# Hybrid decoder step on one Trainium2 core: order of the sample group's memory attention and page attention

## What is computed

```python
# sample group: latent attention over 2048 cached positions in 16 pages of 128 per sequence
q_lat = einsum('bthd,chd->bthc', q_nope, w_uk)
s_past = (q_lat . lat_past + q_rope . kr_past) * scale       # 8 heads, latent 256 + rope 32
p = softmax([s_past, s_new]); o = (p . [lat_past, c_kv]) . w_uv
# sample group: memory attention, 4 heads of 128, 256 memory tokens per sequence
mem_o = softmax(qx . mem_k * X_HEAD_DIM ** -0.5) . mem_v
# both groups
h = x + (g0 * (pool_y @ w_pool_out) + g1 * (mla_o @ w_mla_out) + g2 * (mem_o @ w_x_out)) @ w_o
q = rmsnorm(h) @ w_peer_q; idx, gate = product-key top 16 of 8 heads   # 128 experts per token
y = h + sum_k gate_k * gelu(h . peer_u[idx_k]) * peer_v[idx_k]
```

## Time and profile before

| what | value |
|---|---|
| median of the runs shown | 2406.39 us |
| the profiled execution, its own time | 2412.29 us |
| its span, first to last instruction | 2410.6 us |
| granted TensorE clock, mean | 0.749 |
| moved by DMA | 688.02 MB, mean 285 GB/s |
| instructions | 22105 |

### The profile page before, as it was taken

One profiled execution on the slowest core, in us unless ns is written; L12 is line 12 of the kernel. 1 busy time (PEld: TensorE's weight loads), 2 busy tenths in 40 slices (PEclk: granted clock), 3 DMA queues, 4 the chain that ended last, 5 costly groups with the idle time before them and its releaser, 6 DMA issues.

```text
span 2410.6 us, 22105 instructions
## 1 busy us (share of the span) xinstructions
PE 1353.5 (56%) x7122; PEld 803.3 (33%) x7122; DVE 1138.8 (47%) x2797; ACT 302.5 (13%) x760; POOL 1082.1 (45%) x1182
## 2 busy tenths in 40 slices
PE   7998999894454347998743855500045510034513
PEld 5874788783232224555531611100001100001100
DVE  2104521136757743434798074078866068840060
ACT  2214520112222121001010110000000000000000
POOL 0000000005564534555466156666666676666673
PEclk9998899996776658999865876655566755567656
DMA  6212045437786979999999579999999999999996
GB/s 197 76 57 59 1 111 147 147 107 273 252 293 223 362 277 364 353 370 374 345 389 402 180 275 364 362 391 372 373 345 353 370 384 379 369 348 358 371 384 258
DMA packets 328363, 688.02 MB, mean 285 GB/s; under 512 B 39943, under 2 KB 179528, under 8 KB 328239
## 3 DMA queue, kind: packets, MB, share of 16 engines
q0 software_dynamic: 160032, 576.69, 63.6%
q1 hardware_dynamic: 168215, 109.90, 15.7%
HBM read 682.36 MB, written 4.18 MB: 285 GB/s over the span
## 4 chain that ended last, share of the span: by engine, by line
PE 34%; DVE 23%; issue 12%; another core or an unknown queue 11%; DMA 8%; POOL 5%; DVEq 3%; ACT 2%; SPq 2%; POOLq 0%; ACTq 0%
PE bank L693 26%; DVE arena L1883 15%; POOL arena L640 5%; DVEq L1819 3%; PE bank L1175 3%; PE bank L689 2%; DMA arena<-in_w_mla_out_dram 2%; DMA arena<-in_peer_v_dram,arena 2%; DMA arena<-in_cache_mem_v_dram 1%; DMA arena<-in_x_sample_dram 1%; PE bank L1150 1%; DMA arena<-in_w_pool_out_dram 1%; ACT arena L1211 1%; DVE arena L1826 1%
## 5 line engine op out<-in xcount | busy, mean ns | idle before, releaser
L640 POOL DMA_INDIRECT arena<-in_peer_u_dram,arena x544 | 514.9, 947 | 842.1 <-PE bank L693 548.1
L693 PE MATMUL bank<-arena 128*128 128x256 f32 (+7 forms) x2940 | 706.1, 397 | 103.1 <-issue 52.0
L640 POOL DMA_INDIRECT arena<-in_peer_v_dram,arena x544 | 516.2, 949 | 405.6 <-PE bank L1175 159.3
L1883 DVE CUSTOM_DVE_ANT_0 arena<-arena,bank 128x1024 f32<-128x1024 f32 x544 | 639.2, 1216 | 58.5 <-issue 50.8
L693 PEld LDWEIGHTS bank<-arena 128*128 128x128 f32 (+2 forms) x2940 | 539.2, 192 | 270.2 <-issue 103.5
L1175 PE MATMUL bank<-arena 128*32 128x512 f32 x2176 | 383.4, 842 | 317.5 <-DMA arena<-in_peer_v_dram,arena 251.4
L689 PE MATMUL bank<-arena 128*128 128x128 f32 (+5 forms) x774 | 150.3, 344 | 586.3 <-DVE arena L1900 367.2
L689 PEld LDWEIGHTS bank<-arena 128*128 128x128 f32 (+5 forms) x774 | 115.0, 176 | 636.2 <-DVE arena L1900 368.4
L1175 PEld LDWEIGHTS bank<-arena 128*32 128x32 f32 x2176 | 80.3, 136 | 597.9 <-issue 597.8
L1211 ACT ACTIVATE arena<-bank 128x256 f32<-128x256 f32 (+12 forms) x399 | 156.6, 428 | 505.1 <-PE bank L693 143.5
L1912 DVE TENSOR_TENSOR arena<-arena,bank 128x1024 f32<-128x1024 f32 x5 | 6.1, 1221 | 380.7 <-PE bank L1175 194.8
(11 more groups left out here) (142 smaller groups left out, 777.2 us busy)
## 6 DMA issues: line engine op xcount, KB each, us to landing
arena<-in_w_in_dram SPq DMA_DIRECT2D x48, 512.0 KB
arena<-in_w_peer_q_dram SPq DMA_DIRECT2D x32, 512.0 KB
arena<-in_cache_kv_latent_dram SPq DMA_DIRECT2D x86, 128.0 KB
arena<-in_peer_u_dram,arena POOLq DMA_INDIRECT x544
arena<-in_peer_v_dram,arena POOLq DMA_INDIRECT x544
arena<-in_w_o_dram SPq DMA_DIRECT2D x8, 1024.0 KB
arena<-in_w_in_dram SPq DMA_DIRECT2D x6, 1024.0 KB
arena<-in_cache_kv_latent_dram POOLq DMA_DIRECT2D x42, 128.0 KB
```

What stands on the lines that cost most here:

```text
L640: pool.indirect_dma_start(out=ring[s % RING], out_offset=None, in_=table[0], in_offset=IndirectOffsetOnAxis(ap=ix, axis=0)).then_inc(land[ ...
L693: last = pe.matmul(dst, lhs(k), rhs(k), start=(k == 0), stop=(k == n - 1))
L1883: dve.tensor_tensor_reduce(ring[s % RING], ring[s % RING], h_dot, 1.0, 0.0, ALU.mult, ALU.add, act_a[:, p % 2, k:k + 1]).then_inc(u_free, 1)
```

## The change

1. The memory attention of the 8 samples leaves the background. It now stands behind prompt_kv and ahead of the prompt's attention on TensorE, ScalarE and VectorE, and the prompt's attention waits for its end. It has 3 buffers instead of 2, loaded before the weights of part(0); a load from the fourth on waits for mem_values of the sequence that had the buffer. mem_turns(n+1) stands ahead of mem_values(n-1).
2. In the background only the pages are left ahead of part(1). page_turns(0) and its copies come first; step s then has the units (1) page_probs(s-1) and page_scores(s), (2) page_turns(s+1) with ScalarE's copies, (3) page_values(s-1), and on ScalarE step s's exponential, now behind step s+1's copies. The page buffers and what their loads wait for are as before.
3. SyncE loads 6 pages of a step and GpSimd 2, these ahead of gather 9 + 6s; GpSimd reads both page numbers at once. w_uv moves behind the last page load, into latT's place, once the last scores are done.
4. The ticks: page units 2 gathers apart (3 to 103), part(1)'s merges from 114 on, 5/2 apart, its last unit at 339 instead of 359. zw is cleared at gather 130 instead of 124.

The diff, cut to its core (the mem_ functions themselves are moved unchanged but for `% 2` becoming `% 3` on smem):

```diff
-    return (mine, []) if s < 2 else (mine[0:5], mine[5:])
+    return (mine, []) if s < 2 else (mine[0:6], mine[6:])
...
-    ticks = [u0 + 3 + 5 * i // 3 for i in range(3 * (STEPS + 1))]
-    ticks += [u0 + 90 + 2 * i for i in range(3)]
-    ticks += [u0 + 96 + 2 * i for i in range(2 * (NB + 2))]
-    ticks += [u0 + 138 + 13 * h // 5 for h in range(2 * MERGE)]
-    ticks += [u1 + 11 + 2 * r for r in range(12)]
-    ticks += [u1 + 37 + 2 * t for t in range(3)]
-    ticks += [u1 + 44 + 5 * t // 2 for t in range(3)]
-    ticks += [u1 + 52 + 3 * j for j in range(QJ + 2)]
+    ticks = [u0 + 3 + 2 * i for i in range(3 * (STEPS + 1))]
+    ticks += [u0 + 106 + 2 * i for i in range(3)]
+    ticks += [u0 + 114 + 5 * h // 2 for h in range(2 * MERGE)]
+    ticks += [u0 + 236 + 5 * r // 2 for r in range(12)]
+    ticks += [u1 + 12 + 2 * t for t in range(3)]
+    ticks += [u1 + 20 + 3 * t for t in range(3)]
+    ticks += [u1 + 32 + 3 * j for j in range(QJ + 2)]
...
             def load_memory(b):
-                if b < 2:
-                    sp.wait_ge(pv_mm, STEPS - 2 + b)
-                else:
-                    sp.wait_ge(mo_mm, b - 1)
-                    sp.wait_ge(mt_mm, 2 * (b - 1))
+                if b == 0:
+                    sp.wait_ge(pool_mm, 2 * PG)
+                    sp.wait_ge(pool_d, PG)
+                elif b >= 3:
+                    sp.wait_ge(mo_mm, b - 2)
+                    sp.wait_ge(mt_mm, 2 * (b - 2))
...
+            for b in range(NB):
+                load_memory(b)
             for n in range(4):
                 load_merge(0, n)
...
-                if s == 1:
-                    sp.dma_start(wuvs[:], ...)
-            for b in range(NB):
-                load_memory(b)
+            sp.wait_ge(ps_mm, STEPS)
+            sp.dma_start(wuvs[:], ...)
...
+            pe.wait_ge(kv_ev, KV_UNITS)
+            mem_turns(0)
+            pe.wait_ge(bank_zero, 2)
+            for n in range(NB + 2):
+                if n >= 2:
+                    mem_out(n - 2)
+                if 1 <= n <= NB:
+                    mem_probs(n - 1)
+                if n < NB:
+                    mem_scores(n)
+                if n + 1 < NB:
+                    mem_turns(n + 1)
+                if 1 <= n <= NB:
+                    mem_values(n - 1)
...
             pe.wait_ge(kv_ev, KV_UNITS)
+            pe.wait_ge(mx_ev, NB)
             pe.wait_ge(krk_done, 1)
...
+                page_turns(0)
                 for s in range(STEPS + 1):
                     if s == HALVES + 1:
                         page_out(0)
-                    if s < STEPS:
-                        page_turns(s)
-                    yield
                     if s >= 1:
                         page_probs(s - 1)
                     if s < STEPS:
                         page_scores(s)
+                    yield
+                    if s + 1 < STEPS:
+                        page_turns(s + 1)
                     yield
                     if s >= 1:
                         page_values(s - 1)
```

More of the change, by code:

```diff
@@ L378, in hybrid_step @@
         ld_pagp = [sem(f"ld_pagp{i}") for i in range(3)]
-        ld_smem = [sem(f"ld_smem{i}") for i in range(2)]
+        ld_smem = [sem(f"ld_smem{i}") for i in range(3)]
         ld_wuv = sem("ld_wuv")
@@ L846, in _, with mem_turns @@
                 prompt_kv(n)
+            def mem_turns(b):
+                pe.wait_ge(ld_smem[b % 3], 32 * (b // 3 + 1))
+                for i in range(2):
+                    if b >= 1:
+                        pe.wait_ge(mt_ev, 2 * b - 1 + i)
+                    for k in range(4):
+                        h, m = 2 * i + k // 2, k % 2
+                        last = turn(bank[:, 4 + i, k * P:(k + 1) * P],
+                                    smem[b % 3][:, 0, m, h * XD:(h + 1) * XD], P)
+                    last.then_inc(mt_mm, 1)
@@ new lines, in mem_scores, with mem_out @@
+            def mem_scores(b):
+                pe.wait_ge(mt_ev, 2 * b + 2)
+                if b >= 1:
+                    pe.wait_ge(ms_exp, b)
+                for h in range(XH):
+                    last = pe.matmul(bank[32 * h:32 * h + TS, 6, 0:MEM],
+                                     qxs[:, h, b * TS:(b + 1) * TS], smT[:, h], start=True, stop=True)
+                last.then_inc(ms_mm, 1)
+            def mem_out(b):
+                pe.wait_ge(mo_ev, b + 1)
+                if b >= 1:
+                    pe.wait_ge(mx_ev, b)
+                turn(bank[:, 7, 384:512], smo[:, b % 2], P).then_inc(mx_mm, 1)
@@ new lines, in mem_probs, with mem_values @@
+            def mem_probs(b):
+                pe.wait_ge(ms_exp, b + 1)
+                if b >= 1:
+                    pe.wait_ge(mo_ev, b)
+                if b >= 2:
+                    pe.wait_ge(mx_ev, b - 1)
+                for m in range(2):
+                    last = turn(bank[:, 7, m * P:(m + 1) * P], sms[:, b % 2, m * P:(m + 1) * P], P)
+                last.then_inc(mp_mm, 1)
+            def mem_values(b):
+                pe.wait_ge(mp_ev, b + 1)
+                if b >= 1:
+                    pe.wait_ge(mx_ev, b)
+                for m in range(2):
+                    for h in range(XH):
+                        last = pe.matmul(bank[32 * h:32 * h + TS, 7, 256:256 + XD], smpT[:, m, 32 * h:32 * h + TS],
+                                         smem[b % 3][:, 1, m, h * XD:(h + 1) * XD], start=(m == 0), stop=(m == 1))
+                last.then_inc(mo_mm, 1)
@@ L987, in page_out, with pages @@
                 last.then_inc(po_mm, 1)
[L989 to L1027, removed]
-                    pe.wait_ge(mx_ev, b)
-                for m in range(2):
-                    for h in range(XH):
-                        last = pe.matmul(bank[32 * h:32 * h + TS, 7, 256:256 + XD], smpT[:, m, 32 * h:32 * h + TS],
-                                         smem[b % 2][:, 1, m, h * XD:(h + 1) * XD], start=(m == 0), stop=(m == 1))
-                last.then_inc(mo_mm, 1)
-            def sample():
+            def pages():
                 pe.wait_ge(pq_ev, QJ)
                 pe.wait_ge(sc_ev, QJ)
+                page_turns(0)
                 for s in range(STEPS + 1):
@@ L1067, in sample @@
                 yield
-                pe.wait_ge(bank_zero, 2)
-                for n in range(NB + 2):
-                    if n >= 2:
-                        mem_out(n - 2)
-                    if n < NB:
-                        mem_turns(n)
-                    if 1 <= n <= NB:
-                        mem_probs(n - 1)
-                    yield
-                    if n < NB:
-                        mem_scores(n)
-                    if 1 <= n <= NB:
-                        mem_values(n - 1)
-                    yield
-                pe.wait_ge(mx_ev, NB)
+                pe.wait_ge(sot_ev, 1)
             def part(g):
@@ L1181, in _ @@
                 pass
-            bg = Background(joined(sample(), part(1)))
+            bg = Background(joined(pages(), part(1)))
             for p in range(TILES):
```

147 lines of the change are left out of this document (74 added, 73 removed).

## The result

The changed kernel takes 2516.18 us (median; 2507.39 to 2521.65), against 2406.8 us before (four runs; it was 2406.39 for the first three): a ratio of 1.0451, 95% interval 1.0416 to 1.0486. The forecast was 2467 us, 2408 to 2515. The direction was right, and the time lies just above the range. The profiled execution spans 2519.9 us, 109.3 more than before.

The account below looks back on a forecast made before the run. Gathers were taken to bound the kernel, paced by page steps and these by page loads. Front +62, gather stage +14, part(1) -15 made +61 us: 2473 us against the profiled 2412.3, 2467 at the median; range 2408 to 2515.

Parts of the forecast that it names:

- Part 1, the front: Memory attention moved to the front: five uncovered sequences at 8.75 us plus fill and drain, delaying the first gather 62 us.
- Part 2, the page cycle: Page stage: load, turns, values, load become one cycle, 20.0 us a step against 12.6.
- I take 13.0: Page load on SyncE with a sixth page: 13.0 us from issue until the turns start.
- 4 us each is left: Page stage: VectorE's two picks of about 20 us lie mostly beside loads, leaving 4 us each uncovered.
- they set nothing: ScalarE's page steps: exponential waits behind copies, but probabilities and scores fit inside the next load's 13 us; no cost.
- Two last steps and the start of the stage: Page stage: page_values(0) some 5 us later; two last steps without loads, 15 us; page_values(15) ends at 882.
- The first four merge units lie beside these products: Before tile 0's weights: first four merge units covered by VectorE's 21 remaining products, at about 1.3 us each.
- At its end the ticks are 20 gathers earlier ... I take 3 units: End of part(1): earlier ticks get 3 more query units done before gather 396 stops, saving 15 us.
- (a): Page stage: loads shorten without five gathers' traffic, a step keeps 12.6 us; 2371 us, chance 0.16.
- (b): Page stage and front: load 15.9 us, step 22.9, memory sequences at the old 10.8; 2515 us, chance 0.14.
- (c): Part(1)'s queries finish before gather 396, so its hold vanishes, 38 us less; 2429 us, chance 0.14.
- the signs: Trace marks: first gather near 612 us, TensorE's rope-key wait over 150, turns 18 to 22 apart, gather 396 idle 35 to 45.

Follow-up runs that it names:

- the second experiment: Kernel after with ScalarE's exponential of step s put ahead of the copies of step s + 1, TensorE's turns still ahead of values: 1.0585, 2531.87 us.

## Why the prediction came out as it did

The forecast's mechanism holds: page loads had their lookahead taken away, and the cycle load, turns, values, load sets the step. Undoing that order alone takes 1.0451 to 1.0124. The sum missed by 48 us (+61 said, +109.3 measured, both profiled). Step by step:

- **Part 1, the front: right.** +62 said, +58.3 measured; 8.75 us a sequence said, 8.2 measured. Fill and drain together were as put (18 said, 17 measured), though the "5.2 us from turns to the end of the values" was misread: 854.02 to 859.23 reaches to the next issue, and the values end at 858.56.
- **Part 2, the page cycle: the mechanism right, the load mis-sized.** "I take 13.0" for issue to turns is the step that failed. It measured 16.1 us, in the load shown and in the mean of the twelve loads whose turns show the wait (14.4 to 17.7). The reason beside it, "the engines are emptier", had it the wrong way round: six gathers are released by the same page_values as the load and run in a burst beside it, and with the gathers held back one load takes 10.1 us (761.31 to 771.44). The average DMA share did fall (0.63), but in the 16 us of the load shown it is 0.82, where the three loads of the earlier trace rows had 0.73, 1.04 and 0.88. Turns measured 4.2 (4.6 said), values 2.5 (2.4 said). The 13 steps took 294.5 us where 13 times 20.0 and 8 for the picks had been said: 26 us of the miss.
- **The picks, "4 us each is left": right or better.** In the kernel after no step with a pick stands out, while in the second experiment each does, by 8 to 10 us.
- **The exponential queued behind copies, "they set nothing": right** for the cycle, and more: with turns first, that order keeps the picks off TensorE.
- **Two last steps and the start of the stage: right** within some 2 us each. page_values(15) ends at 970.3; 882 on the old clock is 940 on the new, and the 26 above explain all but 4 of the rest.
- **"The first four merge units lie beside these products": wrong.** 28 us from page_values(15) to the weights were said, 43.8 measured, 16 us of the miss. The units' weights are loaded only when the page stage ends, and TensorE waits 11.3 us for them, ahead of tile 0's weights; VectorE's products stand behind their sums. Moving them away gives some 12 us, and the 30.9 left are close to what was said for the products. I had named the cover and not asked when their weights load.
- **"At its end the ticks are 20 gathers earlier ... I take 3 units": half right by luck.** The gathers' idle time at TensorE's line goes from 59.5 to 52.1, 7 us instead of 15. Moved back, the ticks change nothing. TensorE starts its first query unit at gather 289 instead of 314, and beside gathers a late unit takes some 30 us, so 25 gathers are worth about one unit; two more units were begun before the hold, not three. The "7 in 88 gathers" that I took a rate from were four begun within 16 us (from 1222 us) and then one per 30 to 38 us. From the weights to the end this term and all others behind it came to -8.8 us instead of -15.
- **The rivals.** (a) is out: it needed a step below 15.3 us, and it was 22.65. (b), 2515 us, came nearest, with its load (15.9 said, 16.1 measured) and step (22.9 and 22.65) almost exact; its other half, memory sequences at 10.8 us, was wrong (8.2), and that its total fits is luck: the merge units, which it didn't have, stand in for them. (c) is out: the hold is still there. Of the signs, the first gather, TensorE's wait and the place of page_values came as written; the turns are further apart than the 18 to 22 us said, and the hold is longer than the 35 to 45 said.

Price by part, from the ratios: memory attention in front with its ticks +0.35% (8 us), the step order on top of it +2.2% (about 53 us), the sixth page on SyncE's queue on top of that +2.0% (about 47 us). The last I had put at 1.7 us a step in the load; it costs more than twice that, since it moves the last transfers into the gathers' burst. These prices hold for this order of adding the parts: in the old step order the sixth page costs 0.6% (1.0099 against 1.0035), about 15 us, and with six pages the step order costs 3.5%.

Left open: why instructions come so slowly beside gathers. That it needs the gathers' traffic is shown; what else it needs is not, and whether it is the supply of instructions or the weights' loads was not tried apart. Also open is how the emptied place of the memory attention splits between its stage and the later ones.

## What to carry to other kernels

Where a load waits for the block that frees its buffer, put that block ahead of the one that waits for the next load: here two blocks in the wrong order on TensorE cost 3.3% for the pages (1.0451 against 1.0124), and the same fault some 14 us of the front for the memory loads. Ask of each load what the same release sets off beside it: a wait that keeps the bulk traffic behind a short urgent load made this kernel 1.4% faster. And cover counts only if the covered work's own inputs are there: look when its weights are loaded.

## What the runs showed of the hardware

Beside a burst of six gathers of 512 KB on GpSimd's queue, the turns that wait for SyncE's last small transfer start 5.3 to 8.4 us after its issue (kernel after, twelve loads); with the gathers held back until the load has landed they start 1.7 to 2.7 us after it (eleven loads).

In the kernel after, from the fifth query unit on, TensorE's instructions come mostly one by one, with up to 2.5 us of idle time between, and 12 to 15 us ahead of each unit; a unit takes 30 us, against 4.9 with the gathers stopped. This isn't so wherever gathers fill the DMA engines: beside them, too, the merge units keep TensorE busy 208.9 of 219 us.

A stop of the gathers for 56.6 us shortened their later hold from 52.1 to 4.5 us, and the one execution took 2513.16 us, no more than the kernel after. None of this stands in the prediction.
